# A hybrid decoder step: DeltaNet and the last dense chunk laid out anew on all engines

## The reference, cut to what matters

```
h = h + swiglu(rms_norm(h, f_norm), w_gate, w_up, w_down)
proj = rms_norm(h, b_norm) @ w_in            # q k v (3 x 1024), z (1024), b, a (8 + 8)
q, k, v = silu(causal_depthwise_conv(qkv, conv_w))      # 4 taps
q, k = l2_normalize(q), l2_normalize(k)
beta = sigmoid(b);  g = -exp(a_log) * softplus(a + dt_bias);  gc = cumsum(g)
lower = strict(k k^T * beta * decay)         # 8 heads
u, w = solve(I + lower, [v * beta, k * beta * exp(gc)])  # triangular
v_new = u - w S;  o = q exp(g) S + (q k^T decay) v_new;  S = carried state
o = rms_norm(o, o_norm) * silu(z)
h = h + o @ w_o
```

## Time and profile before

| | |
|---|---|
| median of 3 runs | 1567.47 us (1566.92 to 1569.0) |
| the profiled execution's own time | 1567.38 us |
| its span (first to last instruction) | 1565.4 us |
| PE busy | 1507.0 us, 96% |
| DVE busy | 1204.3 us, 77% |
| ACT busy | 988.8 us, 63% |
| POOL busy | 137.7 us, 9% |
| mean granted TensorE clock | 0.985 |
| read and written in HBM | 438.16 MB, 15.73 MB |

### The profile page before, as it was taken

One profiled execution on the slowest core, in us unless ns is written; L12 is line 12 of the kernel. 1 busy time (PEld: TensorE's weight loads), 2 busy tenths in 40 slices (PEclk: granted clock), 3 DMA queues, 4 the chain that ended last, 5 costly groups with the idle time before them and its releaser, 6 DMA issues.

```text
span 1565.4 us, 22325 instructions
## 1 busy us (share of the span) xinstructions
PE 1507.0 (96%) x8236; PEld 1269.0 (81%) x8236; DVE 1204.3 (77%) x942; ACT 988.8 (63%) x883; POOL 137.7 (9%) x158
## 2 busy tenths in 40 slices
PE   7999999978999899999999999999999999999996
PEld 6878888868988878888888888888888888888884
DVE  6765555546765457889889888888888988988987
ACT  5544333435753536777777777777777777777773
POOL 1021000000314216600000000000000000000100
PEclk9999999988999799999999999999999999999999
DMA  9349555544431125999999999999999999999992
GB/s 372 109 161 375 188 187 189 185 136 135 135 112 53 69 72 216 389 427 384 378 380 386 373 379 380 383 378 378 385 374 380 390 368 384 388 369 364 426 393 86
DMA packets 90540, 454.52 MB, mean 290 GB/s; under 512 B 7665, under 2 KB 8065, under 8 KB 47489
## 3 DMA queue, kind: packets, MB, share of 16 engines
q1 hardware_dynamic: 83696, 430.86, 72.6%
q0 software_dynamic: 6080, 22.29, 3.6%
q10 hardware_dynamic: 720, 0.76, 0.2%
HBM read 438.16 MB, written 15.73 MB: 290 GB/s over the span
## 4 chain that ended last, share of the span: by engine, by line
PE 93%; ACT 3%; DVE 3%; issue 1%; DMA 0%; POOL 0%; POOLq 0%; DVEq 0%; SPq 0%; ACTq 0%
PE PS L327 28%; PE PS L329 28%; PE PS L328 27%; PE PS L1665 2%; DVE w_low L319 1%; ACT w_high L315 1%; PE PS L1179 1%; PE PS L1499 1%; PE PS L1490 1%; PE PS L1546 0%; PE PS L1072 0%; PE PS L1153 0%; PE PS L1693 0%; PE PS L1302 0%; DVE h L1805 0%
## 5 line engine op out<-in xcount | busy, mean ns | idle before, releaser
L319 DVE TENSOR_TENSOR w_low<-w_raw,w_high 128x2048 fp32r<-128x2048 f32 x406 | 931.0, 2296 | 209.2 <-ACT w_high L315 208.7
L315 ACT ACTIVATE w_high<-w_raw 128x2048 fp32r<-128x2048 f32 x406 | 777.8, 1919 | 322.4 <-PE PS L329 317.8
L327 PE MATMUL PS<-w_high,x_high 128*128 128x512 f32 x1264 | 502.2, 397 | 5.3 <-DVE x_low L1813 3.7
L329 PE MATMUL PS<-w_high,x_low 128*128 128x512 f32 x1264 | 494.2, 391 | 0.0
L328 PE MATMUL PS<-w_low,x_high 128*128 128x512 f32 x1264 | 493.5, 390 | 0.0
L327 PEld LDWEIGHTS PS<-w_high,x_high 128*128 128x128 f32 x1264 | 238.2, 188 | 56.2 <-issue 4.3
L329 PEld LDWEIGHTS PS<-w_high,x_low 128*128 128x128 f32 x1264 | 237.9, 188 | 51.0
L328 PEld LDWEIGHTS PS<-w_low,x_high 128*128 128x128 f32 x1264 | 238.2, 188 | 47.1
L327 PE MATMUL PS<-w_high,m_act_high 128*128 128x512 f32 x448 | 175.0, 391 | 1.6 <-DVE m_act_low L2303 1.6
L329 PE MATMUL PS<-w_high,m_act_low 128*128 128x512 f32 x448 | 174.4, 389 | 0.0
L328 PE MATMUL PS<-w_low,m_act_high 128*128 128x512 f32 x448 | 174.3, 389 | 0.0
(11 more groups left out here) (306 smaller groups left out, 1235.8 us busy)
## 6 DMA issues: line engine op xcount, KB each, us to landing
w_raw<-in_m_w_blocks SPq DMA_DIRECT2D x336, 1024.0 KB, 7.1
w_raw<-in_b_w_in SPq DMA_DIRECT2D x16, 1024.0 KB, 5.5
w_raw<-in_f_w_gate SPq DMA_DIRECT2D x14, 1024.0 KB, 5.0
w_raw<-in_f_w_up SPq DMA_DIRECT2D x14, 1024.0 KB, 5.0
w_raw<-in_f_w_down SPq DMA_DIRECT2D x14, 1024.0 KB, 4.8
x_slots_dram<-zeros POOLq DMA_DIRECT2D x12, 512.0 KB, 8.1
w_raw<-in_a_w_qkv SPq DMA_DIRECT2D x5, 1024.0 KB, 18.1
w_raw<-in_a_w_o SPq DMA_DIRECT2D x4, 1024.0 KB, 15.7
```

The lines of the kernel that those rows point to most:

```text
L315: nc.scalar.activation(WH[:, n % SPLIT, :], W[:, n % RAW, :], ACT.Copy).then_inc(hi_done, 1)
L319: nc.vector.tensor_tensor(WL[:, n % SPLIT, :], W[:, n % RAW, :], WH[:, n % SPLIT, :].bitcast(f32), ALU.subtract).then_inc(lo_done, 1)
L327: nc.tensor.matmul(o, sH, mH, start=first, stop=False)
L329: return nc.tensor.matmul(o, sL, mH, start=False, stop=last)
```

## The change

The matmuls and transposes stay the same in number and shape. What changes:

- The dense loops of PE, ACT and DVE run five times instead of six; the rest is written out. The turn of chunk 6 stands between the halves of `down` of chunk 5, and `down` of chunk 6 does token tile 0 first. Its parts have buffers of their own (`f_last_high`, `f_last_low`).
- The norm in front of DeltaNet goes tile by tile. Its gain is loaded as a row (`b_norm`, a new input, broadcast to all partitions on ACT's queue in the dense stage, into the buffer of `u_cross`) and multiplied in by DVE with the root.
- The order of the weight columns is Z0, K0, K1, Q0, V0, V1, Q1, Z1 instead of K0, K1, Q0, Q1, V0, V1, Z0, Z1.
- `conv` is cut into pieces of twelve matmuls (one fourth of a block's columns). First taps, taps and squares come in halves. Squares are one activation of 512 columns, and DVE sums them.
- The inverse of both tiles goes through one pair of banks, 4 and 5 (`INV`). Tile 0 begins while V0's columns are still multiplied, and tile 1 follows one to two levels behind. Pieces of V0, V1, Q1 and Z1, and the turns, key-query and scan of the rest, stand between the operations of a level. Tile 0's scan and outputs stand among tile 1's last levels.
- z's weighting on POOL is done in halves; the last split of an expert block and the norm of the experts' tile 0 move forward.

The dense end and the start on PE:

```diff
-                turned(NC - 1)
-                down(n0 + SUBS_FFN - 2, 0, NC - 1)
+                pe.wait_ge(lo_done, n0 - 3)
+                pe.wait_ge(sem("f_low_done"), 11)
+                down(NC - 2, 0, 0)
+                pe.wait_ge(sem("f_act_done"), 13)
+                last_turned(0).then_inc(sem("f_turn_ps"), 1)
+                pe.wait_ge(sem("f_low_done"), 12)
+                down(NC - 2, 0, 1).then_inc(w_used, 1)
+                pe.wait_ge(lo_done, n0 - 2)
+                down(NC - 2, 1, 0)
+                pe.wait_ge(sem("f_act_done"), 14)
+                last_turned(1).then_inc(sem("f_turn_ps"), 1)
+                down(NC - 2, 1, 1).then_inc(w_used, 1)
+                pe.wait_ge(lo_done, n0 - 1)
+                down(NC - 1, 0, 0)
+                pe.wait_ge(lo_done, n0)
+                down(NC - 1, 1, 0).then_inc(sem("first_tile_ps"), 1)
+                pe.wait_ge(sem("f_low_done"), 14)
+                down(NC - 1, 0, 1).then_inc(w_used, 1)
+                down(NC - 1, 1, 1).then_inc(w_used, 1)
+                pe.wait_ge(xs_done, 2 * norm_no["gdn"] + 1)
+                turn_half(xs, 0, 2, 0).then_inc(sem("tile_ps"), 1)
+                turn_half(xs, 0, 2, 1).then_inc(sem("tile_ps"), 1)
+                pe.wait_ge(sem("tile_low"), 9)
+                gate_piece("Z0", 0, 0, 0)
...
```

DVE at the same place:

```diff
+                last_low_turned(1).then_inc(sem("f_low_done"), 1)
+                split_low(dve, n0)
+                dve.wait_ge(sem("first_tile_ps"), 1)
+                dense_added(0).then_inc(h_done, 1)
+                dve.wait_ge(loaded_gdn, 64)
+                dve.wait_ge(rstd_done, 2 * norm_no["gdn"] + 1)
+                normed_rows(0).then_inc(xs_done, 1)
+                dve.wait_ge(w_used, n0)
+                dense_added(1).then_inc(h_done, 1)
+                dve.wait_ge(sem("tile_high"), 9)
+                turn_low(0, 0, 2).then_inc(sem("tile_low"), 1)
...
```

A stretch of the inverse on PE; the levels' helpers all write bank `INV`:

```diff
+        INV = 4
+        GDN_ORDER = ("Z0", "K0", "K1", "Q0", "V0", "V1", "Q1", "Z1")
...
+                def blocks(lhs, rhs, both=True):
+                    for hh in range(BH):
+                        for s in range(2 if both else 1):
+                            last = nc.tensor.matmul(PS[halves(s), INV + s, HALF * hh:HALF * hh + HALF], lhs(s, hh), rhs(s, hh), start=True, stop=True)
+                    return last
...
+                pe.wait_ge(sem("m_done"), 2)
+                step(0).then_inc(sem("y_ps"), 1)
+                conv("V1", 0, 0, 0)
+                conv("V0", 1, 3, 2).then_inc(w_used, 1)
+                pe.wait_ge(sem("zt_done"), 1)
+                new_inverse_turned(1, 0).then_inc(sem("yn_ps"), 1)
+                key_key(1, 6).then_inc(sem("kk_ps"), 1)
+                pe.wait_ge(sem("y_right"), 1)
+                pe.wait_ge(sem("y_left"), 1)
+                new_inverse(0).then_inc(sem("xn_ps"), 1)
+                conv("V1", 0, 1, 0)
+                conv("V1", 0, 2, 0)
...
```

The rest, from the last z piece on (waits left out here except where a hand-over of the inverse is meant):

```diff
+                gate_piece("Z1", 1, 1, 1).then_inc(w_used, 1)
+                pe.wait_ge(sem("x_done"), 5)
...
+                step(1).then_inc(sem("y_ps"), 1)
...
+                tokens("V0", 0, 6).then_inc(sem("tok_ps"), 1)
+                tokens("V0", 1, 7).then_inc(sem("tok_ps"), 1)
+                pe.wait_ge(sem("zt_done"), 7)
+                new_inverse_turned(4, 0).then_inc(sem("yn_ps"), 1)
...
+                turn_back("Q0", 6).then_inc(sem("tT_ps"), 1)
...
+                key_query(1, 6).then_inc(sem("kq_ps"), 1)
...
+                cross(0).then_inc(sem("cross_ps"), 1)
...
+                new_inverse_turned(4, 1).then_inc(sem("yn_ps"), 1)
...
+                first_outputs(2).then_inc(sem("o_ps"), 1)
...
+                cross(1).then_inc(sem("cross_ps"), 1)
...
+                second_outputs(0).then_inc(sem("o_ps"), 1)
+                pe.wait_ge(sem("tile_low"), 13)
+                project(0, 0, 0, 2)
...
```

Squares on ACT and their sum on DVE:

```diff
-                    for t in range(TT):
-                        for hh in range(4):
-                            last = nc.scalar.activation(tok[:, a, t, h0 + hh, :], PS[:, b + t, 128 * hh:128 * hh + 128], ACT.Square,
-                                                        accum_out=ssq[:, a, t, h0 + hh:h0 + hh + 1])
+                def squares(name, t, bank):
+                    return nc.scalar.activation(tok[:, head_axis(name), t, four_heads(name), :],
+                                                PS[:, bank, :].rearrange("p (n d) -> p n d", d=BD), ACT.Square)
...
+                def sums(name, t):
+                    a, hs = head_axis(name), four_heads(name)
+                    return V.tensor_reduce(ssq[:, a, t, hs], tok[:, a, t, hs, :], AX.X, ALU.add)
```

DVE beside it (one stretch), and the start of the experts:

```diff
+                dve.wait_ge(sem("y_ps"), 5)
+                step_out(1).then_inc(sem("zt_done"), 1)
+                dve.wait_ge(sem("yn_ps"), 4)
+                right(0).then_inc(sem("y_right"), 1)
+                dve.wait_ge(sem("tap0_done"), 11)
+                taps("V1", 1, 1).then_inc(sem("taps_done"), 1)
+                dve.wait_ge(sem("tap0_done"), 12)
+                taps("Q1", 1, 3).then_inc(sem("taps_done"), 1)
+                dve.wait_ge(sem("y_ps"), 6)
+                step_out(0).then_inc(sem("zt_done"), 1)
                 split_low(dve, n0 + 15)
...
-                norm_tile(0)
                 V.tensor_copy(identR[:], ident)
+                split_low(dve, n0)
                 turn_tile("moe", 0)
+                dve.wait_ge(w_used, n0)
+                add_to_h(1, 1, 1).then_inc(h_done, 1)
                 rows_low(0)
-                split_low(dve, n0)
                 choose(0)
```

More of the change, by code:

```diff
@@ L777, in ffn @@
                     silu(n0 + 6, i)
-                    for n in range(9, 12):
+                    for n in blocks:
                         split_high(act, n0 + n, i)
-                turned(NC - 1)
+                with act.Fori(0, NC - 2) as i:
+                    step(i, (9, 10, 11))
+                step(NC - 2, (9,))
             def deltanet(n0):
@@ new lines, in v_evict, with left, new_x @@
+                def v_evict(name, bank):
+                    return nc.scalar.activation(v_tok[:, :, four_heads(name), :],
+                                                PS[:, bank:bank + 2, :].rearrange("p t (n d) -> p t n d", d=BD), ACT.Copy)
+                def left(t):
+                    return nc.scalar.activation(Y[0:HALF, t], half_bank(INV, 0), ACT.Copy)
+                def new_x(l, t):
+                    for s in range(2):
+                        dst = X[halves(s), t] if l < LEVELS - 1 else XF[halves(s), t, :, halves(s)]
+                        last = nc.scalar.activation(dst, half_bank(INV, s), ACT.Copy)
+                    return last
@@ new lines, in gate_sums, with tokens @@
+                def gate_sums():
+                    for i, m in enumerate(("tri", "ones")):
+                        last = nc.tensor.matmul(PS[:, 6, 96 + 16 * i:112 + 16 * i], C(m), gate[:].rearrange("p t h -> p (t h)"),
+                                                start=True, stop=True)
+                    return last
+                def tokens(name, t, bank):
+                    for hh in range(4):
+                        last = nc.tensor.transpose(PS[:, bank, 128 * hh:128 * hh + 128],
+                                                   cv[:, 4 * GDN_COL[name] + hh, 128 * t:128 * t + 128], ident)
+                    return last
@@ new lines, in new_inverse_turned, with new_inverse, cross @@
+                def new_inverse_turned(l, t):
+                    return blocks(lambda s, hh: X[halves(s), t, hh, :], lambda s, hh: Zt[halves(s), t, hh, :], l < LEVELS - 1)
+                def new_inverse(t):
+                    return blocks(lambda s, hh: Zt[halves(s), t, hh, :], lambda s, hh: X[halves(s), t, hh, :])
+                def cross(t):
+                    for hh in range(BH):
+                        last = nc.tensor.matmul(PS[HALF:128, INV, HALF * hh:HALF * hh + HALF], U12[0:HALF, t, hh, :],
+                                                Y[0:HALF, t, hh, :], start=True, stop=True)
+                    return last
@@ new lines, in output_sums, with gated @@
+                def output_sums(t):
+                    return V.tensor_reduce(sso[:, t], k_tok[:, t], AX.X, ALU.add)
+                def gated(t, bank):
+                    for hh in range(BH):
+                        zh = z[:, t, BD * hh:BD * hh + BD]
+                        last = V.scalar_tensor_tensor(out=zh, in0=pair(bank)[:, hh, :], scalar=rso[:, t, hh:hh + 1], in1=zh,
+                                                      op0=ALU.mult, op1=ALU.mult)
+                    return last
```

1376 lines of the change are left out of this document (814 added, 562 removed).

## The result

The changed kernel takes **1543.16 us** (median of 4 runs, 1540.71 to 1543.59) against 1568.24 us for the kernel before on the same chip (4 runs, 1566.92 to 1569.02). The ratio is 0.9838, 95% interval 0.9821 to 0.9855: 25 us faster, where 28.4 were predicted, and 4.2 us above the predicted 1539.0. The profiled execution took 1543.43 us, 1.6 more than its span of 1541.8.

The account below looks back on a forecast made before the run. TensorE bounds the stretch: 218.8 us of full-clock work plus 1.4 + 2.6 + 5.6 idle and 6.3 slow clock gives 234.7 against 263.1. So 1567.4 - 28.4 = 1539.0 us, 8 in 10 for 1532 to 1557.

Parts of the forecast that it names:

- The compared stretch: From the dense loop's last down to the end of DeltaNet's second output projection: 263.1 us before, predicted 234.7.
- Dense end to z: From dense end to z's first piece: TensorE idle falls from 9.5 to 1.4 us, with no slow clock expected.
- just hidden: Tile 0's adds, square, root and normalised row, about 5 us, fit under the 5.4 us by which its down ends earlier.
- Convolutions and inverse under pieces: Convolution pieces beside the inverse's first seven chains cover its hand-overs, leaving 2.6 us idle; before, 8.8.
- costed at nothing: Side effects given no cost, including POOL's reordered maps; three POOL meetings stretching a DVE split on a chain would cost 4 us.
- The rest: After the last piece to the first projection: 40.6 us of TensorE work, a 46 us chain, so 5.6 us idle.
- 218.8 us stays: TensorE's full-clock work in the stretch stays 218.8 us, since every matmul and transpose keeps its shape.
- The clock: Cross block and work beside it ran 13.5 us at half clock before; that 6.3 us cost was kept whole.
- The first: Half of the work after the last piece runs at 1.2 GHz: 20.3 us instead of 6.3, total 1553.0 us; chance 0.22.
- third: From the last z piece to the first projection TensorE stays at 1.2 GHz: 40.6 us more, 1573 us; chance 0.05.
- The second: A third of 28 hand-overs through the one bank pair slip 2.3 us behind splits: 21 us more, 1560; chance 0.08.
- The fourth: The new order brings nothing: TensorE waits as much as before because lists align badly, 1567 us; chance 0.03.

Follow-up runs that it names:

- the run with both tiles together: Changed kernel with chunk 6's down ordered half 0 of both tiles, then half 1 of both: 1547.37 us, ratio 0.9856 to the kernel before.
- the alternated run: Changed kernel plus 16 unread extra pieces and 16 groups of 64 x 64 blocks before z's turn, by turns instead of grouped: 1585.37 us (grouped 1584.38).
- the artificial waits: Changed kernel with three or eight extra DVE self-copies before the cross block's subtraction of tile 0: 1546.54 us with three, 1550.66 us with eight.
- grouped pieces: Changed kernel with five pieces of V1, Q1 and Z1 moved from between the inverse's operations into groups: 1550.19 us, ratio 0.9873.

## Why the prediction was right, and where its terms were off

The forecast case came true: no slow clock in the rest, no slipping, 25 us faster. By its steps:

- **The compared stretch** carries the difference: 24.9 of 25 us by the medians. The experts' part keeps PE at 300.00 of 300.00.
- **Dense end to z**: predicted a gap of 1.4 us; the window 341.40:359.30 has 1.2 idle and the dense end none. The chain "just hidden" is shown by the run with both tiles together (2.24 of 2.7 us uncovered), and its worth by the run with the norm for both tiles (10 us). The turns between the halves are worth 1.3 us besides. Correct in size, and in mechanism for the norm. Of the 3.6 us idle at 329.10:334.20, which I put down to the turns' place, 2.58 were the wait for chunk 5's adds; they went because the adds are left out.
- **Convolutions and inverse under pieces**: predicted 2.6 idle, measured 121.96 - 117.26 = 4.7. 3.1 of them are the two waits for POOL's masks, which I had under "costed at nothing"; the other 1.6 are waits on DVE and lie under the 2.6. I had the meeting of POOL and DVE the wrong way round: I priced a DVE split stretched by POOL and not a POOL mask held up by a DVE split, 3.96 and 3.38 for 1.3 us. With 1.3 neither wait would have been there (an estimate from the rows above: 2.7 and 2.1 us less against waits of 2.3 and 0.8). Moving one piece ahead took 1.4 of the 2.3 back.
- **The rest**: predicted 46 us with 5.6 idle, measured 49.7 with 4.8 idle; PE was busy 44.9 and not 40.6. The idle time was nearly right, the work 4.3 us short. By kinds, the sum had 13.0, 16.3, 5.4 and 6.0 for the inverse, the 128-column groups, the transposes and the cross block; the trace has 15.4, 17.8, 7.3 and 4.4. I had also counted six groups of eight transposes where the window holds seven (z's turn), about 0.9 us, and had the cross block too dear.
- **"218.8 us stays"** is the term that was mis-sized most: 225.5. The stretch of before changes 12 times between 64-wide blocks and wider operations, the new one 62 times. 50 x 0.17 = 8.4 us by the alternated run, against 6.7 measured (7.1 on equal work). That price was measured beside 256-column pieces, which are only 22 of the 62; 33 are beside 128-column groups, whose price no run has by itself. I had taken every duration from inside a run, 0.93 to 0.98 for a group of blocks and 1.44 for a piece, for groups that now stand alone at 1.08 and 1.63.
- **The clock**: 6.3 kept, 1.7 measured, and in the other place: none in the rest, where I kept it, and one stretch among the convolutions, where I had expected none. I had tied the 13.5 us stretch to the kind of operation; the artificial waits tie its beginning to the wait in front: in the kernel after, these operations ran at the higher clock, and behind a wait of 3.0 us at the lower. In the kernel before a wait stood there too:

```profile
528.59 1.97 PE L1521 MATMUL PS<-cst,tok 128*128 128x128 f32 x8 [2.35 <-ACT cv L921]
```

  Its length is not explained: behind 2.35 us of waiting PE worked 12.5 us at the lower clock, behind 3.0 and 6.6 us only 6.3.
- **Rivals.** The first and third (half or all of the rest at 1.2 GHz) fell: 481.26:530.93 is at 1.00. The rule of the Trainium skill that spoke for the first (TensorE: Matmul & The Clock Gate, Part 4: PE-mode transpose: transposes don't count as activity the way matmuls do) does not agree with these runs: neither 56 transposes in the window of the rest nor 80 in a row lowered the clock. The second, hand-overs that slip behind splits, would have been 21 us; all waits of the inverse on DVE sum to 2.4 + 0.9 + 0.8. The fourth fell with the waits of 5.8 and 4.9.

The two errors of the sum, +6.7 of work and -4.6 of clock, partly cancelled, which is luck; with 1.4 of idle the stretch came out 3.5 us long, and the other 0.7 of the 4.2 us lie outside it.

## What to carry to other kernels

Going tile by tile through a norm, so that one tile's chain lies under the other's matmuls, and laying independent pieces between the steps of a dependent chain are worth what the lists say, wait by wait: undoing the first cost 10 us here, and undoing the second for five pieces 5.5. But count the changes of shape that such an order makes, and price them (0.17 us between 64 x 64 blocks and 128-row matmuls here). And look at the engine that seems idle: a short POOL operation beside a DVE weight split took three times its time and became the largest wait of the new order. Beside other DVE operations it took its usual 1.3 us.

## What the runs showed of the hardware that I had not expected

- A slow stretch is not tied to one place. Behind the same wait of 2.3 us on POOL it came in the kernel after and most runs, and not with both tiles' down together or with grouped pieces; behind the 0.8 us wait before the cross block's second product it came in the runs with transposes and with the norm for both tiles, and not in the kernel after. The single ones are 3.4 us long and cost 1.4 to 1.7 us, as much as the medians here differ by. What decides it stays open.
- After a change from 64 x 64 blocks the first wide matmul took 0.39 us and not 0.28, here in the kernel after:

```profile
450.58 0.28 PE L342 MATMUL PS<-x_high,w_low 128*128 128x256 f32 x1
450.79 1.15 PE L1555 MATMUL PS<-invT,u_level 64*64 64x64 f32 x32
451.87 0.39 PE L340 MATMUL PS<-x_high,w_high 128*128 128x256 f32 x1
452.09 0.28 PE L341 MATMUL PS<-x_low,w_high 128*128 128x256 f32 x1
```

  The piece before it also ends 0.21 us after its last start, where 0.12 is the pitch.
- DVE's copy of 128 x 1024 from SBUF to SBUF took 0.72 us; products of the same size with a PSUM operand took 1.22.
